# A two-block transformer kernel on one core: who rounds the pooled parts, who copies the queries' columns, where one weights' split stands, and filler products at the beginning

## The chip, the core and the metric

The kernel runs on one core of a Trainium2 chip. The core's engines work from queues of their own: TensorE (PE, with its weight loads shown as PEld), VectorE (DVE), ScalarE (ACT), GpSimd (POOL) and SyncE (SP, which here only issues transfers). They meet at semaphores. The metric is the time of the whole program in microseconds (us), and lower is better.

## What is computed

The program is two blocks, one after the other, on 512 tokens of width 1024. The first block is a gated feed-forward, a mixer and another gated feed-forward. The mixer is what the change touches:

```python
h = rms_norm(x, mix_norm[l])
proj = h @ w_in[l]
q, k, v, qi, ki, wi, u = jnp.split(proj, split_points, axis=-1)
q = rope(rms_norm(q.reshape(B, S, N_HEADS, HEAD_DIM), q_norm[l]), pos, HEAD_DIM)
k = rope(rms_norm(k.reshape(B, S, N_HEADS, HEAD_DIM), k_norm[l]), pos, HEAD_DIM)
attn = dsa_attention(q, k, v, qi, ki, wi, top_k)      # softmax over the 128 best keys by qi, ki, wi
pooled = jnp.einsum('bsgc,gcd->bsgd', multiscale_pool(u), pool_w[l])
pooled = pooled.reshape(B, S, POOL_WIDTH) * pool_scale[l]
x = x + jnp.concatenate([attn, pooled], axis=-1) @ w_out[l]
```

The second block (two attentions with gates, then a convolved feed-forward) is left as it was. All data are 32-bit floats; the large products are made of three products of a high and a low part, which need both operands rounded (the high part) and their remainders (the low part).

## The kernel before

**Weights.** They come through four slots of 1024 columns. SP loads a slab into `raw`, ACT rounds it into `wH` (`split`, L1757 to L1768), POOL makes the remainder `wL` (L806), and PE multiplies. A product of stage and slab needs all three.

**The beginning.** PE waits for the identity matrix and a gain vector, transposes the first half of `x` (L1092, 4 transposes for each of 4 token tiles, each tile when its transfer has landed), then multiplies 4 feature tiles (`first_slabs`). For each feature tile `k` ACT makes the high part (L1804) and DVE the low part (L2310) and a copy of `x` (L2306). PE goes on to the second half of `x` and its four feature tiles. POOL fills constants first, `ones` among them (L794).

**The first attention** has 32 units, `n = 8 * tile + head`. Each engine walks the same units in program order, written by hand (`first_attention` on PE, ACT and DVE):

- PE at an even unit makes the logits of units n+2 and n+3 (`logit_pair`); then it turns the probabilities of unit n (`turn`, L1455), multiplies those of unit n-1 with the values, and runs its `during1(n)`.
- ACT takes the exponential of unit n+1 (L1954), copies the turned probabilities of unit n out of PSUM (L1971), and runs its `during1(n)`.
- DVE masks the logits of unit n+2 (L2613); at units 9, 17 and 25 it normalises the tile before (L2634, L2636); then it runs its `during1(n)`. There it also picks the best keys of the last tile at every even unit from 2 to 20 (`pick`, L2561 and L2562).

In `during1` stand two side jobs. **Pooled parts:** `POOL_AT = {1: 0, 6: 1, 9: 2, 14: 3}` says at which unit PE makes pooled product g into PSUM bank 5 (`pool_product`). ACT rounds it into `hidH` at the same unit (`pool_high`, L1939), and DVE makes the remainder `hidL` two units later (`pool_low`, L2590). All four products use bank 5, and so the next one, and every turn of queries into bank 5, waits for the remainder of the one before (semaphore `hid_ready`). **Tiles of queries and keys:** at units 4, 12 and 20 (`TILE_TURN`) PE turns the next tile's queries and keys (L1405), and ACT copies both out of PSUM, the queries' columns first and the keys' second (`tile_columns`, L1935). The next tile's logits wait for both.

At unit 9 ACT also splits the last slab (slot 3) of the weights that follow the attention (`out1`).

Of the kernel before, what the change touches and what calls it, by code (L numbers as in the profile page):

```python
# [143 lines left out]
def _build(nc, t, stack):  # L144
# [229 lines left out]
    def sem(name):  # L374
        return stack.enter_context(nc.semaphore(name))
# [39 lines left out]
    exp_begun = sem("exp_begun")  # L415
    qk_sq, qk_rot, qk_T, qk_out = sem("qk_sq"), sem("qk_rot"), sem("qk_T"), sem("qk_out")
    att_qk, q2_rot, q2_T, q2_hi, q2_lo, k2_hi = (sem(n) for n in ("att_qk", "q2_rot", "q2_T", "q2_hi", "q2_lo", "k2_hi"))
# [138 lines left out]
    def highs_to(what, n):  # L556
# [40 lines left out]
                   ("conv_w2", t["conv_w_2"][0, 2])]  # L597
    VEC_DMAS = len(vec_sources) - 1

    def prob_of(n):  # L600
# [369 lines left out]
    def _(pe):  # L970
# [120 lines left out]
        def x_block(k, q):  # L1091
            return nc.tensor.transpose(bank(X_BANK[k], P, q * P), xnat[:, q * D + k * P:q * D + (k + 1) * P], ident)  # L1092

        pe.wait_ge(const_in, 16)
        pe.wait_ge(gain_in, 16)
        nc.tensor.transpose(bank(1, KT), vec_rows[0:KT, 0:P], ident[0:KT, 0:KT]).then_inc(gain_T, 1)
        for q in range(ST - 1):
            pe.wait_ge(x_in[q], 16)
            for k in range(4):
                x_block(k, q)  # L1100
        pe.wait_ge(x_in[ST - 1], 16)
        for k in range(4):
# [273 lines left out]
        def before_v():  # L1376
            pe.wait_ge(drained_a, drain_base["k"] + 4)
            pe.wait_ge(k_scaled, 1)

        def pool_product(g):  # L1380
            if g < 2:
                pe.wait_ge(v_late, g + 1)
            if g == 0:
                pe.wait_ge(pooled, 4)
                pe.wait_ge(misc_in, MISC_DMAS * 16 + 16)
            if g >= 1:
                pe.wait_ge(hid_ready, NF + g)
                pe.wait_ge(qk_out, (2, 4, 4, 6)[g])
            product(bank(POOL_BANK[g]), pool_w[:, g * P:(g + 1) * P], u_pool[:, g * S:(g + 1) * S],
                    True, True).then_inc(pool_mm, 1)  # L1390

        def tile_turn(q):
            if q:
                pe.wait_ge(qk_out, 2 * q)
            if q > 1:
# [17 lines left out]
        def during1(n):  # L1413
# [5 lines left out]
            if n in EARLY_TURN:  # L1419
                if EARLY_TURN[n] == 0:  # L1420
                    pe.wait_ge(hid_ready, NF + 4)
                    pe.wait_ge(attn_out, GROUPS1 - 1)
                    pe.wait_ge(qk_out, 2 * ST)
                attn1_turn(EARLY_TURN[n], range(ST - 1))
# [11 lines left out]
        def logit_pair(n):  # L1436
            if n >= 4:
                pe.wait_ge(logit, n - 2)
            if n % NH == 0:
                pe.wait_ge(qk_out, 2 * (n // NH + 1))  # L1440
            for u in group1[n:n + 2]:
# [301 lines left out]
    def _(act):  # L1743
# [185 lines left out]

        def tile_columns(q):  # L1930
            into = (qT1[:, q % 2 * 4 * P:][:, 0:4 * P].rearrange("p (a s) -> p a s", a=4),
                    kT1[:].rearrange("p (a s) -> p a s", a=4)[:, :, q * P:(q + 1) * P])
            for n, b in enumerate(TURN1_BANK[q]):
                act.wait_ge(qk_T, 2 * q + n + 1)
                nc.scalar.activation(into[n], bank(b).rearrange("p (a s) -> p a s", a=4), ACT.Copy).then_inc(qk_out, 1)  # L1935

# [5 lines left out]
        def during1(n):  # L1942
            if n in TILE_TURN:
                tile_columns(TILE_TURN[n])
            if n in POOL_AT:
                pool_high(POOL_AT[n])
            if n == 9:
                split(stage_of["out1"], 0, SLOTS - 1)
# [8 lines left out]
        def first_units():  # L1957
            tile_columns(0)
            exps(0)
            exps(1)  # L1960
# [300 lines left out]
    def _(dve):  # L2261
# [331 lines left out]
        def during1(n):  # L2593
            if n - 2 in POOL_AT:
                pool_low(POOL_AT[n - 2])
            if n in PICK_AT:
                pick(3, 6 + PICK_AT.index(n), 7 + PICK_AT.index(n))
# [566 lines left out]
```

## Time and profile before

| | |
|---|---|
| median of 3 runs | 1738.71 us (1737.01 to 1739.12) |
| the profiled execution's own time | 1738.32 us |
| its span, first to last instruction | 1736.5 us |
| busy: PE / PEld / DVE / ACT / POOL | 98% / 80% / 56% / 38% / 54% |
| share of the last-ended chain on PE | 91% |
| span of the first attention's units | about 507.6 to 562 us |

### The profile page before, as it was taken

The page shows a single profiled execution, that of the slowest core. Times are in us where ns is not written, and L with a number is a line of the kernel's source. Part 1 is how long each engine was busy: PE and PEld are TensorE (multiplying, and loading weights), DVE is VectorE, ACT ScalarE, POOL GpSimd, SP SyncE. Part 2 cuts the span into 40 slices and gives each one's busy share as a digit, 9 for nine tenths or more (in the row PEclk, how much of TensorE's full clock was granted, in tenths as well). Part 3 has the DMA queues.
Part 4 walks back from the last instruction along what each step waited for, and adds up shares of the span by engine and source line. Part 5 has one row for each costly group of instructions (what it writes and reads, how often), then busy time and mean ns, then how long its engine had stood idle before and what let it go on. Part 6 is the DMA issues. An engine that isn't in the chain of part 4 may idle for free.

```text
span 1736.5 us, 24431 instructions
## 1 busy us (share of the span) xinstructions
PE 1705.2 (98%) x8123; PEld 1388.1 (80%) x8123; DVE 977.5 (56%) x1507; ACT 665.8 (38%) x1382; POOL 930.2 (54%) x755
## 2 busy tenths in 40 slices
PE   8999999999999999999999999999999999999997
PEld 7888888888777888888888888864478988888887
DVE  4258645768985467352123529578767673542544
ACT  5322222343466433223223323665632642332333
POOL 4554453567982445544444545467943755544541
PEclk9999999999999999999999999999999999999998
DMA  7354452534211346523423433100122234333321
GB/s 236 109 179 148 146 158 85 176 93 133 73 49 49 122 146 189 150 86 98 126 83 86 122 97 89 33 1 25 49 61 85 71 93 140 97 97 98 97 85 49
DMA packets 279967, 178.39 MB, mean 103 GB/s; under 512 B 6537, under 2 KB 258629, under 8 KB 279749
## 3 DMA queue, kind: packets, MB, share of 16 engines
q1 hardware_dynamic: 265620, 149.36, 29.9%
q10 hardware_dynamic: 14256, 27.87, 4.7%
q8 instruction: 52, 0.85, 0.2%
q14 instruction: 39, 0.31, 0.1%
HBM read 175.11 MB, written 2.10 MB: 102 GB/s over the span
## 4 chain that ended last, share of the span: by engine, by line
PE 91%; DVE 5%; ACT 1%; issue 1%; DMA 1%; POOL 1%; SPq 0%; DVEq 0%; ACTq 0%; POOLq 0%
PE ps L973 89%; DVE mod_acc L2345 2%; PE ps L1455 1%; DVE stat L2662 0%; DVE ps L2688 0%; PE ps L1280 0%; DMA mod_raw<-in_w_mod 0%; DMA xnat<-in_x 0%; POOL wL L806 0%; PE ps L1660 0%; ACT prob2B L2091 0%; POOL actL L860 0%; DVE x L2388 0%; PE ps L1405 0%; PE ps L1154 0%
## 5 line engine op out<-in xcount | busy, mean ns | idle before, releaser
L806 POOL TENSOR_TENSOR wL<-raw,wH 128x512 fp32r<-128x512 f32 (+2 forms) x560 | 747.4, 1358 | 709.1 <-ACT wH L1768 698.1
L973 PE MATMUL ps<-actH,wH 128*128 128x512 f32 (+1 forms) x1312 | 510.6, 389 | 2.6 <-POOL actL L860 1.9
L973 PE MATMUL ps<-actH,wL 128*128 128x512 f32 (+1 forms) x1312 | 503.6, 384 | 0.0
L973 PE MATMUL ps<-actL,wH 128*128 128x512 f32 (+1 forms) x1248 | 480.0, 385 | 0.0
L1768 ACT ACTIVATE wH<-raw 128x512 fp32r<-128x512 f32 (+2 forms) x558 | 311.1, 608 | 295.5 <-PE ps L973 295.4
L973 PEld LDWEIGHTS ps<-actH,wH 128*128 128x128 f32 x1312 | 247.1, 188 | 53.5 <-issue 2.4
L973 PEld LDWEIGHTS ps<-actH,wL 128*128 128x128 f32 x1312 | 246.4, 188 | 49.1
L973 PEld LDWEIGHTS ps<-actL,wH 128*128 128x128 f32 x1248 | 235.1, 188 | 46.7 <-DVE actL L2310 0.8
L973 PE MATMUL ps<-hidH,wH 128*128 128x512 f32 (+1 forms) x720 | 267.6, 372 | 0.0
L973 PE MATMUL ps<-hidH,wL 128*128 128x512 f32 (+1 forms) x720 | 266.6, 370 | 0.0
L973 PE MATMUL ps<-hidL,wH 128*128 128x512 f32 (+1 forms) x720 | 266.5, 370 | 0.0
L973 PEld LDWEIGHTS ps<-hidH,wL 128*128 128x128 f32 x720 | 135.6, 188 | 23.2
L973 PEld LDWEIGHTS ps<-hidH,wH 128*128 128x128 f32 x720 | 135.7, 188 | 23.0
L973 PEld LDWEIGHTS ps<-hidL,wH 128*128 128x128 f32 x720 | 135.7, 188 | 22.8
L2345 DVE SCALAR_TENSOR_TENSOR mod_acc<-mod_raw,silu_c,mod_acc 128x512 f32<-128x512 f32 x112 | 119.5, 1067 | 3.9
L1841 ACT ACTIVATE sg<-g 128x512 f32<-128x512 f32 x44 | 27.8, 632 | 209.7 <-DVE g L2368 209.7
L2370 DVE TENSOR_TENSOR ur<-ps,rB 128x512 f32<-128x512 f32 x44 | 30.3, 690 | 123.4 <-PE ps L973 123.4
L973 PE MATMUL ps<-wH,actH 128*128 128x512 f32 (+1 forms) x224 | 85.2, 381 | 0.0
L973 PE MATMUL ps<-wL,actH 128*128 128x512 f32 (+1 forms) x224 | 84.7, 378 | 0.0
L973 PE MATMUL ps<-wH,actL 128*128 128x512 f32 (+1 forms) x224 | 84.6, 378 | 0.0
L1845 ACT ACTIVATE hidH<-h 128x512 f32 (+1 forms) x44 | 27.7, 630 | 127.2 <-DVE h L2373 127.2
L2388 DVE SCALAR_TENSOR_TENSOR x<-ps,x 128x512 f32 (+1 forms) x32 | 21.6, 690 | 88.0 <-PE ps L973 86.8
(378 smaller groups left out, 2039.8 us busy)
## 6 DMA issues: line engine op xcount, KB each, us to landing
mod_raw<-in_w_mod ACTq DMA_DIRECT2D x24, 1024.0 KB, 6.1
raw<-in_w_in SPq DMA_DIRECT2D x48, 512.0 KB, 3.7
raw<-in_ffn_w_up SPq DMA_DIRECT2D x44, 512.0 KB, 3.8
raw<-in_w_up SPq DMA_DIRECT2D x44, 512.0 KB, 3.9
raw<-in_ffn_w_gate SPq DMA_DIRECT2D x43, 512.0 KB, 3.8
raw<-in_ffn_w_down SPq DMA_DIRECT2D x32, 512.0 KB, 4.0
raw<-in_w_out SPq DMA_DIRECT2D x16, 512.0 KB, 3.8
raw<-in_w_down SPq DMA_DIRECT2D x16, 512.0 KB, 3.8
```

The source lines that it names most:

```text
L806: nc.gpsimd.tensor_tensor(wL[:, b:b + w // 2], raw[:, b:b + w // 2], wH[:, b:b + w // 2].bitcast(F32), ALU.subtract).then_inc(lo_ready, 1)
L973: return nc.tensor.matmul(out, a, b, start=first, stop=last)
L1455: mm = nc.tensor.transpose(into, prob_of(n)[:, b * P:(b + 1) * P], ident)
L1768: nc.scalar.activation(wH[:, b:b + w // 2], raw[:, b:b + w // 2], ACT.Copy).then_inc(hi_ready, 1)
L1841: nc.scalar.activation(sg[:], g1[:], ACT.Silu).then_inc(silu_ready, 1)
L1845: nc.scalar.activation(tile(hidH, f), h[:], ACT.Copy).then_inc(h_high, 1)
L2345: ins = V.scalar_tensor_tensor(o, w, s, o, ALU.mult, ALU.add)
L2370: V.tensor_tensor(ur[:], bank(2 * q + 1), rB[:], ALU.mult).then_inc(drained_v, 1)
L2388: V.scalar_tensor_tensor(tile(x, m), bank(j), 0.5, tile(x, m), ALU.mult, ALU.add).then_inc(drained_v, 1)
```

## The change

1. At the beginning PE makes products of `ones` with `ones` into bank 3, which nobody reads: six before it waits for the identity matrix, and one after each of the first three token tiles' transposes.
2. ACT rounds a pooled part one unit later (`n - 1 in POOL_AT`), and DVE makes its remainder one unit later (`n - 3`). PE makes the products at the same units as before.
3. At units 4, 12 and 20 DVE copies the queries' columns, and ACT the keys' alone. The first tile stays with ACT. The semaphore `qk_out` becomes two, `q_cols` and `k_cols`.
4. The split of slot 3 moves from unit 9 to unit 22.

```diff
+        def awake(n):
+            for _ in range(n):
+                product(bank(3, P), ones[:], ones[:], True, True)
+
+        pe.wait_ge(cleared, 2)
+        awake(6)
         pe.wait_ge(const_in, 16)
...
             for k in range(4):
                 x_block(k, q)
+            awake(1)
         pe.wait_ge(x_in[ST - 1], 16)
...
+        def columns_out(tiles):
+            pe.wait_ge(q_cols, tiles)
+            pe.wait_ge(k_cols, tiles)
...
             if g >= 1:
                 pe.wait_ge(hid_ready, NF + g)
-                pe.wait_ge(qk_out, (2, 4, 4, 6)[g])
+                columns_out((1, 2, 2, 3)[g])
...
-        def tile_columns(q):
-            into = (qT1[:, q % 2 * 4 * P:][:, 0:4 * P].rearrange("p (a s) -> p a s", a=4),
-                    kT1[:].rearrange("p (a s) -> p a s", a=4)[:, :, q * P:(q + 1) * P])
-            for n, b in enumerate(TURN1_BANK[q]):
-                act.wait_ge(qk_T, 2 * q + n + 1)
-                nc.scalar.activation(into[n], bank(b).rearrange("p (a s) -> p a s", a=4), ACT.Copy).then_inc(qk_out, 1)
+        def key_columns(q):
+            act.wait_ge(qk_T, 2 * q + 2)
+            nc.scalar.activation(kT1[:].rearrange("p (a s) -> p a s", a=4)[:, :, q * P:(q + 1) * P],
+                                 bank(TURN1_BANK[q][1]).rearrange("p (a s) -> p a s", a=4), ACT.Copy).then_inc(k_cols, 1)
...
         def during1(n):
             if n in TILE_TURN:
-                tile_columns(TILE_TURN[n])
-            if n in POOL_AT:
-                pool_high(POOL_AT[n])
-            if n == 9:
+                key_columns(TILE_TURN[n])
+            if n - 1 in POOL_AT:
+                pool_high(POOL_AT[n - 1])
+            if n == 22:
                 split(stage_of["out1"], 0, SLOTS - 1)
...
         def during1(n):
-            if n - 2 in POOL_AT:
-                pool_low(POOL_AT[n - 2])
+            if n - 3 in POOL_AT:
+                pool_low(POOL_AT[n - 3])
+            if n in TILE_TURN:
+                q = TILE_TURN[n]
+                dve.wait_ge(qk_T, 2 * q + 1)
+                V.tensor_copy(query_columns(q), bank(TURN1_BANK[q][0])).then_inc(q_cols, 1)
             if n in PICK_AT:
                 pick(3, 6 + PICK_AT.index(n), 7 + PICK_AT.index(n))
```

PE at the beginning, after the change (before it, the rows with `ones` are missing and the 16 transposes stand in one row; `const` is the identity matrix):

```order
L978 MATMUL ps<-ones 128x128 x6
L1107 MATMUL ps<-const,vec_rows 128x8
L1097 MATMUL ps<-const,xnat 128x128 x4
L978 MATMUL ps<-ones 128x128
L1097 MATMUL ps<-const,xnat 128x128 x4
L978 MATMUL ps<-ones 128x128
L1097 MATMUL ps<-const,xnat 128x128 x4
L978 MATMUL ps<-ones 128x128
L1097 MATMUL ps<-const,xnat 128x128 x4
```

Nine products were added, all ahead of the last four transposes.

DVE in the first attention before, from the logits of unit 10 (written to `prob_1`, in the program's unit 8) to the pick of unit 10. `hidL` is the remainder of a pooled part, here of part 1; `small` and `work` belong to the pick; `RECIPROCAL` and `attn` are the normalising of tile 0:

```order
L2613 ISA prob_1_106,stat<-ps,work 128x256
L2613 ISA stat 128x1
L2590 SCALAR_TENSOR_TENSOR hidL<-ps,cols,hidH 128x512
L2561 MAX small<-work 128x8
L2562 MATCH_REPLACE work<-small,work 128x512
L2613 ISA prob_2_107,stat<-ps,work 128x256
L2613 ISA stat 128x1
L2634 RECIPROCAL stat<-stat 128x8
L2636 TENSOR_TENSOR attn_104<-ps,stat 128x512
L2613 ISA prob_0_105,stat<-ps,work 128x256
L2613 ISA stat 128x1
```

The same place after the change:

```order
L2633 ISA prob_1_106,stat<-ps,work 128x256
L2633 ISA stat 128x1
L2577 MAX small<-work 128x8
L2578 MATCH_REPLACE work<-small,work 128x512
L2633 ISA prob_2_107,stat<-ps,work 128x256
L2633 ISA stat 128x1
L2654 RECIPROCAL stat<-stat 128x8
L2656 TENSOR_TENSOR attn_104<-ps,stat 128x512
L2606 SCALAR_TENSOR_TENSOR hidL<-ps,cols,hidH 128x512
L2633 ISA prob_0_105,stat<-ps,work 128x256
L2633 ISA stat 128x1
```

The remainder of part 1 moved behind a pick, the logits of unit 11 and both instructions of the normalising.

ACT before, from the exponential of unit 10 (in the program's unit 9) to that of unit 12. `hidH` is the rounding of part 2, `wH` the split of slot 3:

```order
L1954 ACTIVATE prob_1_106,stat<-prob_1_106,stat 128x256
L1971 ACTIVATE probT_108<-ps 128x256
L1939 ACTIVATE hidH<-ps,cols 128x512
L1768 ACTIVATE wH<-raw 128x512 x2
L1954 ACTIVATE prob_2_107,stat<-prob_2_107,stat 128x256
L1971 ACTIVATE probT_108<-ps 128x256
L1954 ACTIVATE prob_0_105,stat<-prob_0_105,stat 128x256
```

And after the change:

```order
L1968 ACTIVATE prob_1_106,stat<-prob_1_106,stat 128x256
L1987 ACTIVATE probT_108<-ps 128x256
L1968 ACTIVATE prob_2_107,stat<-prob_2_107,stat 128x256
L1987 ACTIVATE probT_108<-ps 128x256
L1953 ACTIVATE hidH<-ps,cols 128x512
L1968 ACTIVATE prob_0_105,stat<-prob_0_105,stat 128x256
```

The rounding moved behind one exponential and one copy, and the two halves of the split are gone from here.

## Rows read from the trace of the kernel before

**Rows 1.** The page: span, and busy time of each engine.

```profile
span 1736.5 us, 24431 instructions
PE 1705.2 (98%) x8123; PEld 1388.1 (80%) x8123; DVE 977.5 (56%) x1507; ACT 665.8 (38%) x1382; POOL 930.2 (54%) x755
```

**Rows 2.** Timeline at the beginning: start us, length us, engine, instruction [idle before].

```profile
1.22 0.20 POOL L794 MEMSET ones<- 128x128 f32 x1
4.05 0.24 PE L1096 MATMUL ps<-const,vec_rows 8*128 8x8 f32 x1 [4.05 <-DMA vec_rows<-in_ffn_norm]
7.18 0.71 PEld L1092 LDWEIGHTS ps<-const,xnat 128*128 128x128 f32 x4 [0.54 <-DMA xnat<-in_x]
7.76 0.69 ACT L1804 ACTIVATE actH<-ps,gain 128x512 fp32r<-128x512 f32 x1 [3.25 <-PE ps L1092]
...
9.74 2.06 DVE L2310 SCALAR_TENSOR_TENSOR actL<-ps,gain,actH 128x512 fp32r<-128x512 f32 x3
...
11.72 1.88 DVE L2306 COPY x<-ps 128x512 f32<-128x512 f32 x3
...
13.90 2.42 ACT L1804 ACTIVATE actH<-ps,gain 128x512 fp32r<-128x512 f32 x4 [1.24 <-PE ps L1092]
```

**Rows 3.** Timeline of PE at the change of its clock.

```profile
12.41 0.63 PE L973 MATMUL ps<-actL,wH 128*128 128x512 f32 x1
12.84 2.33 PE L1092 MATMUL ps<-const,xnat 128*128 128x128 f32 x16
14.93 1.18 PE L973 MATMUL ps<-actH,wL 128*128 128x512 f32 x4
```

**Rows 4.** Stretches: length, busy us of PE PEld DVE ACT POOL, granted clock, DMA.

```profile
525.70:529.11 3.41, 3.41 (x18) 3.32 (x17) 1.89 (x7) 2.02 (x6) 3.41 (x3) 0.50 0.69 207
522.29:525.70 3.41, 2.14 (x17) 1.63 (x17) 2.83 (x9) 2.82 (x10) 3.41 (x4) 1.00 0.00 1
```

**Rows 5.** Timeline of DVE, units 8 and 9 of the first attention.

```profile
518.30 0.75 DVE L2590 SCALAR_TENSOR_TENSOR hidL<-ps,cols,hidH 128x512 fp32r<-128x512 f32 x1
...
521.05 0.69 DVE L2636 TENSOR_TENSOR attn<-ps,stat 128x512 f32<-128x512 f32 x1
```

**Rows 6.** Timeline of PE, units 9 to 14.

```profile
520.15 1.08 PE L973 MATMUL ps<-u_pool,pool_w 128*128 128x512 f32 x2
521.16 0.70 PE L973 MATMUL ps<-kT,qT 64*128 64x256 f32 x4
...
523.89 0.41 PE L1455 MATMUL ps<-const,prob 128*128 128x128 f32 x2 [1.27 <-ACT probT L1971]
...
526.12 1.06 PE L1405 MATMUL ps<-const,q 128*128 128x128 f32 x4
...
529.14 0.92 PE L973 MATMUL ps<-kT,qT 64*128 64x384 f32 x4
```

**Rows 7.** Timeline of ACT, units 9 to 12.

```profile
521.26 0.69 ACT L1939 ACTIVATE hidH<-ps,cols 128x512 fp32r<-128x512 f32 x1 [0.92 <-PE ps L973]
521.85 1.14 ACT L1768 ACTIVATE wH<-raw 128x512 fp32r<-128x512 f32 x2
...
523.38 0.37 ACT L1971 ACTIVATE probT<-ps 128x256 f32<-128x256 f32 x1
...
528.08 0.60 ACT L1935 ACTIVATE kT<-ps 128x512 f32<-128x512 f32 x1 [0.26 <-PE ps L1405]
```

**Rows 8.** Timelines of PE and DVE, units 16 and 20 to 24.

```profile
533.47 0.52 PE L1455 MATMUL ps<-const,prob 128*128 128x128 f32 x3 [0.28 <-ACT probT L1971]
...
540.70 0.61 PE L1405 MATMUL ps<-const,q 128*128 128x128 f32 x4
...
540.29 0.69 DVE L2561 MAX8 small<-work 128x8 f32<-128x512 f32 x1
...
542.26 0.56 DVE L2613 CUSTOM_DVE_ANT_0 prob<-ps,work 128x384 f32<-128x384 f32 x1
...
547.03 0.66 PE L1455 MATMUL ps<-const,prob 128*128 128x128 f32 x4
```

More of the change, by code:

```diff
@@ L415, in _build @@
     exp_begun = sem("exp_begun")
-    qk_sq, qk_rot, qk_T, qk_out = sem("qk_sq"), sem("qk_rot"), sem("qk_T"), sem("qk_out")
+    qk_sq, qk_rot, qk_T = sem("qk_sq"), sem("qk_rot"), sem("qk_T")
+    q_cols, k_cols = sem("q_cols"), sem("k_cols")
     att_qk, q2_rot, q2_T, q2_hi, q2_lo, k2_hi = (sem(n) for n in ("att_qk", "q2_rot", "q2_T", "q2_hi", "q2_lo", "k2_hi"))
@@ L598, in _build, with query_columns @@
     VEC_DMAS = len(vec_sources) - 1
+    def query_columns(q):
+        return qT1[:, q % 2 * 4 * P:][:, 0:4 * P]
     def prob_of(n):
@@ L1393, in tile_turn @@
             if q:
-                pe.wait_ge(qk_out, 2 * q)
+                columns_out(q)
             if q > 1:
@@ L1422, in during1 @@
                     pe.wait_ge(attn_out, GROUPS1 - 1)
-                    pe.wait_ge(qk_out, 2 * ST)
+                    columns_out(ST)
                 attn1_turn(EARLY_TURN[n], range(ST - 1))
@@ L1439, in logit_pair @@
             if n % NH == 0:
-                pe.wait_ge(qk_out, 2 * (n // NH + 1))
+                columns_out(n // NH + 1)
             for u in group1[n:n + 2]:
@@ L1957, in first_units @@
         def first_units():
-            tile_columns(0)
+            act.wait_ge(qk_T, 1)
+            nc.scalar.activation(query_columns(0), bank(TURN1_BANK[0][0]), ACT.Copy).then_inc(q_cols, 1)
+            key_columns(0)
             exps(0)
```

## The prediction, made before the changed kernel had run

> **What bounds the kernel now.** I read the page first: PE is busy for 98% of the span, with some 31 us of idle time in all [rows 1]. So a change in the time is a change in PE's idle time, in PE's work, or in PE's clock. Then I read the timeline in the two places that the change touches.
>
> At the beginning PE first works at 4.05 us, and DVE paces it: the low parts of feature tiles 1 to 3 run without a pause from 9.74 to 11.80, then three copies until 13.60 [rows 2]. PE is on its low level all that time. The product at 12.41 and what follows it at 12.84 lie 0.43 us apart, while four products from 14.93 take 1.18 us, with the tail of the last in it, or 0.25 us each [rows 3]. Half of the clock of 2.4 GHz is 1.2 GHz, so the level rose during the 16 transposes between, after PE had worked without a pause since 9.0 us.
>
> In the first attention PE has many small waits. Two stand out. The turn of unit 11 comes at 523.89 after 1.27 us of idleness [rows 6], because ACT had the rounding of pooled part 2 (itself 0.92 us waiting for PE's product) and then 1.14 us of split ahead of the exponential and the copy that PE needs [rows 7]. And in the stretch from 525.70 to 529.11 the granted clock is 0.50, 1.2 GHz, after a stretch in which PE had been busy for 2.14 of 3.41 us [rows 4].
>
> **Part 1, the filler.** `ones` is there at 1.42 [rows 2]. A plain 32-bit product stands in the trace as two passes (the pooled product is `x2` [rows 6]), and I take a pass of 128 columns to be as long as a transpose of 128 columns. Four transposes take 1.06 us at 1.2 GHz and 0.61 at 2.4, the tail of the last, some 0.2 us, with them [rows 6, 8], so that one is 0.215 or 0.108 us. So six products are 12 passes, 12 x 0.215 = 2.6 us, from 1.5 to 4.1. The first useful transpose comes at 4.05 today [rows 2], so they cost at most 0.1 us, and the wait for the transfers of `x` hides that. The three single ones add 3 x 0.43 = 1.3 us. Today PE waits 0.54 us for the last token tile, until 7.18 [rows 2]. If the clock stays low, the last four transposes begin near 8.1 instead, 0.9 us late. If it rises near 6.9, what is left then runs in half the time, and they begin near 7.5, 0.15 to 0.3 us late. I take that: today the rise came after 4.7 us without a pause (9.0 to 13.7), and with the filler PE has none from 1.5 on.
>
> What that buys: DVE's low parts are no faster, so the eighth product can begin no sooner than 11.80 plus the delay of 0.15, and ends at 12.2 instead of 12.84. The 16 transposes take 16 x 0.108 = 1.7 instead of 2.1 us. The first four of them are done at 12.6, so ACT's high part of feature tile 4 moves from 13.90 [rows 2] to 12.75, and DVE's low part to the end of its copies, 13.75, instead of 14.62. PE then stays just behind DVE and is done with this slab 1.2 us sooner. Behind it PE has no idle time worth naming until the modulation chain at 103 us, whose transfer is issued behind PE's work, so that nothing there holds the gain back. Term: -1.2 us, with ends -1.4 (rise at once) and +0.9 (no rise).
>
> **Parts 2 and 4, the pooled parts and the split, units 5 to 11.** What ACT gives back is plain: no rounding and no split between unit 10's work and unit 11's. But bank 5 is one bank. PE's product of part 2, at unit 9, may not start before DVE has made the remainder of part 1. Today that is done at 519.05 and the product begins at 520.15 [rows 5, 6], 1.1 us later. After the change the remainder stands behind the normalising, whose last instruction ends at 521.74 today [rows 5]. The remainder's 0.7 us leave the time ahead of that. The copy of the queries' columns at unit 4 comes in, at 0.65 us, like the three copies that take 1.88 us together [rows 2]. DVE also waits for it there, so that its later instructions are at best where they are now. So the remainder begins near 521.7 and ends near 522.4: PE waits from 520.3 to 522.45. **This is a new wait of 2.1 us.** Behind it on PE stand the pair of logits (1.01 us after the product's start), the turn of unit 10 (0.63 later, 0.4 long like that of unit 11), ACT's copy of it (0.51 from its start to PE's next turn [rows 6, 7]), and then the turn of unit 11: 522.45 + 1.01 + 0.63 + 0.45 + 0.51 = 525.1, against 523.89 today [rows 6, 7]. So the 1.27 us that the split cost are gained, and 1.2 us more than that are lost: +1.2 us at this point. The bounds: 0 if DVE came out of unit 4 so early that the remainder is done by 521.3, and +2.1 if nothing of the split's time came back.
>
> **Part 3, the columns of tiles 2 and 3.** At tile 2 the turn starts 1.2 us later, at 527.4 instead of 526.12 [rows 6]. At 2.4 GHz its eight transposes take 0.9 us instead of 1.7, and ACT copies only the keys, 0.60 us [rows 7], right behind them: the logits of tile 2 can begin at 527.4 + 0.9 + 0.15 (tail) + 0.60 + 0.15 = 529.2, as today (529.14). The lateness is made good here, as far as the clock is high. At unit 16 PE waits 0.28 us for ACT today, behind the rounding of part 3 [rows 8]; that goes: -0.3. At tile 3 the copy on DVE stands ahead of the last pick and of the logits of unit 23. It can't start before the queries are turned, near 541.0 (540.70 + 0.61 less 0.3 [rows 8]); 0.65 for it, and the 1.97 us that the pick and the closing of the mask take today (540.29 to 542.26 [rows 8]) put those logits at 543.6 instead of 542.26. ACT's exponential of unit 23 can then begin at 544.2. Behind it stand a copy, now the two halves of the split (1.14 us), the exponential of unit 24 and the copy of unit 23, four pieces of 0.4 to 0.8 us besides the split, 3.6 us in all, and PE's turn of unit 24 comes at about 547.8 instead of 547.03 [rows 8]: +0.75 us at the end, and from there to the end of the attention PE and ACT take turns without slack. The other user of the split is POOL, whose 2.5 us for slot 3 then end near 549 to 551; PE needs them past 562, so that is hidden. Term for all of the attention at a high clock: +0.75 us, with ends -0.6 and +2.1.
>
> A rule of the Trainium skill bears on the copy. (VectorE: DVE Perf Modes, Why PSUM operands drop a tier, says that an fp32 operand in PSUM holds VectorE to one element a cycle. 512 columns at that page's 0.96 GHz are 0.53 us by estimate, and the rows of like copies agree roughly at 0.63 to 0.69; by the page's figure the term would be 0.1 us smaller.)
>
> **The clock in the attention.** Before, the fall to 1.2 GHz followed one idle time of 1.27 us with small ones around it. Now one of 2.1 us stands a little ahead of that place. I expect a fall again, within some us behind 520.3, and as long as today's, 3.4 us. It takes up to 1.7 us of work from PE; some 0.5 us of that falls into waits that are left. Today's fall is in today's time and I have taken it out above (the turns at tile 2). Term: +1.2 us, with ends 0 and +1.7.
>
> **Sum.** -1.2 + 0.75 + 1.2 = +0.75. The profiled execution took 1738.32 us (span 1736.5 [rows 1]), 0.4 below the median of 1738.71, so that the changed kernel comes to **1739.1 us**.
>
> **Rivals.** (a) *The clock does not fall behind the new wait:* -1.2 + 0.75 = -0.45, 1737.9 us. For it: other waits of 0.4 to 0.9 us on PE in this stage bring no fall today, and the new one comes in one piece with busy work around it. Against: today one of 1.27 us sufficed [rows 4, 6]. (b) *The filler does not lift the clock in time*, so that part 1 doesn't do what it is there for: +0.6 instead of -1.2 (0.9 us late, 0.3 of it back because the later transposes run high): 1740.9 us. For it: the products use only the same constant, and PE may have pauses where the token tiles land late. (c) *The new wait isn't there*, because DVE is early enough at unit 9: then the split's 1.27 us and the fall of the clock (some 1.1 us) are gained as well: 1738.32 - 1.2 - 2.4 = 1734.7 us. Against it stands the order: one pick, one masking and the normalising lie ahead of the remainder, and the normalising ends at 521.74 today. (d) *Slower:* the clock stays at 1.2 GHz or goes to and fro through units 9 to 20, since PE and ACT wait for each other there. Each us at that level costs 0.5; the bound of a measurable loss (3.5 us) is passed at 8 us of low clock, and at 10 us the time is 1737.9 + 5 = 1742.9 us. Against it: today the level came back within 3.4 us, with PE busy throughout [rows 4]. (The Trainium skill bears on this one: TensorE: Matmul & The Clock Gate, A second HAM failure mode, tells of a kernel whose small idle times between groups of products made the clock go to and fro. The trace agrees in one fall, and shows no second.)
>
> **How the numbers follow.** Chances: forecast 0.50, (a) 0.20, (b) 0.12, (c) 0.06, (d) 0.07, anything else 0.05. A measurement of this kernel can tell some 0.2%, 3.5 us, from no change: below 1735.2 is faster, above 1742.2 slower. The forecast, (a) and (b) lie within it. Faster is (c) with a part of the rest, 0.06; slower is (d) and a part of (b), 0.09; the same 0.85. The range of 8 in 10 runs from (a) with a gain of 1.4 us more (the ends of the attention's term) to (b) with half a microsecond: 1736.5 to 1741.4.
>
> **What would show it.** The filler: rows of `ones` from 1.5 to 4.1, transposes 0.11 us apart before the last token tile, and the second half's transposes near 12.2. The new wait: PE idle for some 2 us ahead of the third pooled product, ended by DVE's `hidL`. No split between unit 9 and 11. The clock: a stretch of 0.50 behind that wait. Logits of unit 23 about 1.3 us later against the turn of tile 3. I am wrong if PE has no wait ahead of the third product, if the first attention as a whole isn't 0 to 3 us longer than before, or if the first 100 us are not about 1 us shorter.

## The result, and the profile after

| | before | after |
|---|---|---|
| median | 1738.64 us (1735.45 to 1743.14, 21 runs) | 1741.86 us (1739.22 to 1745.25, 21 runs) |
| ratio after to before | | 1.0017, 95% interval 1.0011 to 1.0023 |
| the profiled execution's own time | 1738.32 us | 1744.24 us |
| its span | 1736.5 us | 1742.5 us |

The changed kernel is slower by 3.0 us on the mean (1.9 to 4.0 by the interval), and by 3.2 us by the medians. That is 0.17%, so it lies inside what the prediction called the same, but the interval does not reach down to no change. The forecast was 1739.1, and the median is 0.5 us above the range that went with it.

The page after, span and busy time, in the columns of [rows 1]:

```profile
span 1742.5 us, 24471 instructions
PE 1711.2 (98%) x8141; PEld 1391.1 (80%) x8141; DVE 978.2 (56%) x1510; ACT 664.2 (38%) x1379; POOL 929.1 (53%) x755
```

PE's busy time and the span both grew by 6.0 us, so that PE is idle for as long as before, 31.3 us. A part of the added busy time is the filler, which stands where PE used to be idle. The rest is work that took longer, and the stretches below show where the clock was low.

**The beginning, after.** PE's timeline, as in [rows 2, 3]:

```profile
1.48 2.93 PE L978 MATMUL ps<-ones 128*128 128x128 f32 x12 [1.48 <-POOL zero L800]
4.34 0.27 PE L1107 MATMUL ps<-const,vec_rows 8*128 8x8 f32 x1
...
7.42 0.60 PE L1097 MATMUL ps<-const,xnat 128*128 128x128 f32 x4
9.06 0.50 PE L978 MATMUL ps<-actH,wH 128*128 128x512 f32 x1 [1.03 <-ACT wH L1815]
...
12.24 1.91 PE L1097 MATMUL ps<-const,xnat 128*128 128x128 f32 x16
...
20.13 0.39 PE L978 MATMUL ps<-actH,wL 128*128 128x512 f32 x1
21.30 0.66 PE L1092 MATMUL ps<-const,vec_rows 128*128 128x128 f32 x4 [0.78 <-DMA vec_rows<-in_conv_w]
```

`vec_rows` holds the constant vectors, which arrive in 15 small transfers. This went as forecast up to the last row. The twelve passes run from 1.48 to just past 4. The granted clock rises at 6.33 us instead of 13.7, and the last token tile's transposes take 0.60 us without a wait. The second half of `x` is turned at 12.24 (forecast: near 12.2; before: 12.84), and by 20 us PE is 1.0 us ahead. Then it waits 0.78 us. The four transposes at the end are those of `vec_rows`, which `vector_turns` puts behind feature tile `k` = 3 of the second slab (`(j, k) == (1, 3)`). Before, they stood there too, at nearly the same time, and without a wait. Here are the same rows of the kernel before:

```profile
21.20 0.39 PE L973 MATMUL ps<-actH,wL 128*128 128x512 f32 x1
21.43 0.60 PE L1087 MATMUL ps<-const,vec_rows 128*128 128x128 f32 x4
21.78 0.48 PE L973 MATMUL ps<-actH,wH 128*128 128x512 f32 x1
```

So 1.0 us of lead became 0.1. It is not that the constants always land just ahead of 21.3 us. The trace records the semaphore updates by which the 15 transfers report that they have landed. The last one recorded came at 19.53 us before, 1.9 us ahead of PE, and PE 1.2 us sooner would still have come behind it. After the change it came at 21.26, 0.04 us ahead of PE's start, although the last of the transfers was issued at 17.8 us in both. (A trace can miss some of the updates.) One thing that differs around it is a transfer of 16 KB in the queue that the profile calls `instruction`. The first line is from the transfers before, between 23.2 and 25 us, and the second from those after, between 18.9 and 20.4:

```profile
q8 instruction: 1, 0.02, 4.0%
q8 instruction: 1, 0.02, 3.6%
```

It starts at 23.39 us before and at 19.17 after. The experiments below come back to it.

**The first attention, after.** PE's timeline, units 9 to 11, as in [rows 6]:

```profile
519.34 0.41 PE L1471 MATMUL ps<-const,prob 128*128 128x128 f32 x2 [0.77 <-ACT probT L1987]
519.59 0.56 PE L978 MATMUL ps<-v,probT 128*128 128x64 f32 x4
522.05 2.07 PE L978 MATMUL ps<-u_pool,pool_w 128*128 128x512 f32 x2 [1.91 <-DVE hidL L2606]
524.06 1.23 PE L978 MATMUL ps<-kT,qT 64*128 64x256 f32 x4
525.21 0.69 PE L1471 MATMUL ps<-const,prob 128*128 128x128 f32 x2
525.70 0.95 PE L978 MATMUL ps<-v,probT 128*128 128x64 f32 x4
526.47 0.66 PE L1471 MATMUL ps<-const,prob 128*128 128x128 f32 x2
```

The timeline of DVE at the same place, as in [rows 5]:

```profile
520.42 0.20 DVE L2654 RECIPROCAL stat<-stat 128x8 f32<-128x8 f32 x1
520.65 0.69 DVE L2656 TENSOR_TENSOR attn<-ps,stat 128x512 f32<-128x512 f32 x1
521.26 0.74 DVE L2606 SCALAR_TENSOR_TENSOR hidL<-ps,cols,hidH 128x512 fp32r<-128x512 f32 x1
```

The new wait is there, and for the reason given: the remainder `hidL` stands behind the normalising, and the third pooled product needs bank 5 from it. PE idles for 1.91 us. ACT has neither a rounding nor a split between units 10 and 11 any more, and PE's turn of unit 11, at 526.47, is ready without a wait. But its products are long: the pair of the pooled product takes 2.07 us, and 1.08 in [rows 6]. The stretches say why. Columns are length, busy us of PE, PEld, DVE, ACT and POOL, granted clock, DMA share and GB/s, as in [rows 4]:

```profile
518.33:521.74 3.41, 1.04 (x9) 0.80 (x7) 3.31 (x10) 2.34 (x8) 3.25 (x4) 1.00 0.00 0
521.74:525.15 3.41, 3.10 (x6) 1.01 (x6) 0.26 (x1) 0.00 (x0) 3.41 (x3) 0.50 0.00 0
525.15:528.57 3.42, 3.42 (x18) 2.98 (x16) 2.23 (x7) 2.31 (x7) 3.42 (x4) 0.50 0.65 189
528.57:531.98 3.41, 3.41 (x19) 3.02 (x16) 1.71 (x5) 0.39 (x1) 0.44 (x1) 0.50 0.81 240
531.98:535.40 3.42, 3.25 (x20) 2.07 (x20) 3.32 (x11) 2.81 (x9) 0.00 (x0) 1.00 0.10 31
```

The clock is at 1.2 GHz from 521.74 to 531.98, 10.24 us, and not for 3.4 us as in [rows 4]. PE was busy for all but 0.3 us of that. Against the kernel before, the same instructions are 0.03 us early at 500 us, 0.27 us early at 506 us (just ahead of the attention), 4.32 us late at 560 us (behind it), and as late at 900. A second fall, at 1166.86 in the second block's attention, which the change doesn't touch, adds 1.7.

**Unit 23**, as in [rows 8]. The first row is of DVE, the others of ACT and PE:

```profile
544.82 0.69 DVE L2615 COPY qT<-ps 128x512 f32<-128x512 f32 x1 [0.81 <-PE ps L1421]
...
547.39 0.56 DVE L2633 CUSTOM_DVE_ANT_0 prob<-ps,work 128x384 f32<-128x384 f32 x1
...
548.98 1.14 ACT L1784 ACTIVATE wH<-raw 128x512 fp32r<-128x512 f32 x2
...
549.22 0.52 PE L1471 MATMUL ps<-const,prob 128*128 128x128 f32 x3 [0.91 <-ACT probT L1987]
```

The two rows apart are DVE's copy and the logits of unit 23. The copy takes 0.69 us, the masking of unit 23 begins 2.57 us after its start, 3.2 us behind the turn of tile 3 (1.6 before, [rows 8]), and PE idles 0.91 us ahead of its turn of unit 23. The split comes behind that and delays nothing that PE waits for: its next turn follows without a wait ended by ACT.

### The profile page after: what moved, and what is told of

It reads as the page before. It is cut to its first block, busy times and chain, and to the rows that moved or that the text cites. A ratio compares the mean times of both kernels' runs of the same rounds, so it can differ in the third digit from the quotient of the medians.

```text
span 1742.5 us, 24471 instructions
## 1 busy us (share of the span) xinstructions
PE 1711.2 (98%) x8141; PEld 1391.1 (80%) x8141; DVE 978.2 (56%) x1510; ACT 664.2 (38%) x1379; POOL 929.1 (53%) x755
## 4 chain that ended last, share of the span: by engine, by line
PE 90%; DVE 5%; issue 1%; ACT 1%; SPq 1%; DMA 1%; POOL 1%; DVEq 0%; ACTq 0%; POOLq 0%
PE ps L978 88%; DVE mod_acc L2361 2%; PE ps L1471 1%; DVE stat L2682 0%; DVE ps L2708 0%; PE ps L1292 0%; SPq L752 0%; DMA mod_raw<-in_w_mod 0%; SPq L773 0%; POOL wL L811 0%; PE ps L1421 0%; PE ps L1676 0%; ACT prob2B L2107 0%; POOL actL L865 0%; DVE x L2404 0%
## 5 line engine op out<-in xcount | busy, mean ns | idle before, releaser
L978 PEld LDWEIGHTS ps<-hidH,wL 128*128 128x128 f32 x720 | 135.6, 188 | 23.2
L2404 DVE SCALAR_TENSOR_TENSOR x<-ps,x 128x512 f32 (+1 forms) x32 | 21.5, 689 | 88.1 <-PE ps L978 87.3
```

Of the source, the lines that this page charges most:

```text
L978: return nc.tensor.matmul(out, a, b, start=first, stop=last)
L2404: V.scalar_tensor_tensor(tile(x, m), bank(j), 0.5, tile(x, m), ALU.mult, ALU.add).then_inc(drained_v, 1)
```

## The experiments

All numbers of "lead" are differences between the start of the same PE instruction in a kernel's trace and in that of the kernel before; negative is earlier. What the attention costs is read from 506 to 560 us. At 500.07 us PE waits for `q` from DVE, and a kernel that comes there early or late gains or loses up to 0.4 us, which belongs to the stage ahead. Where a kernel has 11 runs, its time stands beside 15 or 33 runs of the kernel before on the same chip.

### The beginning: E1 and E2

E1 is the kernel before with the filler alone. E2 has the filler, and the turns of the constants' rows two feature tiles (six products) later:

```diff
+        pe.wait_ge(cleared, 2)
+        awake(6)
...
-                    if (j, k) == (1, 3):
+                    if (j, k) == (1, 5):
```

> The kernel before with the filler products alone. Theory 1 (the clock rises early and the first half slab is done 1.0 us sooner, but PE then waits for the transfer of the last constant vectors near 21.3 us, ahead of the four transposes of vec_rows, and gives the gain back): transposes of vec_rows at 21.3 to 21.4, time within 0.3 us of before. Rival (the gain of 1.0 us goes through, and what was lost after the change was lost later): 1.0 us less than before.

> The kernel before with the filler, and with the transposes of the constant vectors two feature tiles later on PE. Theory 1: no wait for the constants' transfer, PE is 1.0 us ahead of before at 30 us and still at 95 us, time 1.0 us less than before. Rival (another constraint of the first 100 us holds the beginning, such as the row scale's chain): less than 0.3 us.

Measured: E1 1737.32 us (1736.00 to 1741.13), ratio 0.9996 (0.9987 to 1.0005); E2 1737.21 (1736.43 to 1741.18), 0.9997 (0.9988 to 1.0006). Neither can be told from no change by its time. The traces tell them apart. PE in E1, and then in E2:

```profile
20.14 0.39 PE L973 MATMUL ps<-actH,wL 128*128 128x512 f32 x1
21.38 0.66 PE L1087 MATMUL ps<-const,vec_rows 128*128 128x128 f32 x4 [0.85 <-DMA vec_rows<-in_conv_w]
```

```profile
21.30 0.40 PE L973 MATMUL ps<-actH,wL 128*128 128x512 f32 x1
21.54 0.60 PE L1087 MATMUL ps<-const,vec_rows 128*128 128x128 f32 x4
21.89 0.47 PE L973 MATMUL ps<-actH,wH 128*128 128x512 f32 x1
```

In E1 PE waits 0.85 us at the constants, and its lead at 500 us is -0.03. In E2 it doesn't wait for them, and leads by 1.3 us from 24 us and by 1.5 at 500 us. So in these two the gain is lost at the constants and nowhere else.

The other runs below have the same beginnings, so that all thirteen profiles can be read together. The middle columns are the last recorded landing of the constants and the start of the 16 KB transfer; "lead" is that of PE:

| beginning | profiles | last landing | 16 KB transfer | PE's wait | lead at 20 us | lead at 24 us |
|---|---|---|---|---|---|---|
| no filler | before, E3, E4, E5 | 19.53 to 19.89 | 23.4 to 23.8 | none | -0.46 to +0.33 | -0.48 to +0.33 |
| filler, turns in place | after, E1, E6, E7, E9, E10 | 20.96 to 21.50 | 18.2 to 19.2 | 0.19 to 0.88 | -1.30 to -0.41 | -0.38 to +0.17 |
| filler, turns later | E2, E8, E11 | 19.64 to 19.76 | 19.37 to 19.43 | none | -1.25 to -1.11 | -1.28 to -1.12 |

The filler is worth 0.85 us at 20 us (the mean of nine profiles less the mean of four), a part of it by chance of when the clock rises. With the turns in place nothing of it is left at 24 us, and with the turns later all of it. The constants landed late only where the 16 KB transfer started by 19.2 us, in six profiles of six, and in none of the other seven. That this transfer is PE's code, which the added instructions and the moved turns shift, and that it holds the constants up, fits the rows but is not shown. E2 moved both at once, PE's use of the constants and the 16 KB transfer, and doesn't part them: its constants had landed at 19.64 us, ahead of where PE would have met them without the move.

E2's profile had a fall of the clock in the second attention (at 1159.53), E1's had none. So the profiled executions hide the difference between the two. That the filler makes the kernel faster is not shown by any run's time.

### The parts of the attention, one by one: E3, E4, E5

E3 moves the split alone (`if n == 9` to `if n == 22` in ACT's `during1`). E4 moves the rounding and the remainders of the pooled parts alone (`n - 1 in POOL_AT` on ACT, `n - 3` on DVE). E5 gives the queries' columns to DVE alone:

```diff
+            if n in TILE_TURN:
+                q = TILE_TURN[n]
+                dve.wait_ge(qk_T, 2 * q + 1)
+                V.tensor_copy(query_columns(q), bank(TURN1_BANK[q][0])).then_inc(q_cols, 1)
```

> The kernel before with the split of slot 3 at unit 22 alone. Theory (the split at unit 9 costs 1.27 us of PE's idle time and brings the clock's fall, a further 1 us): 1.0 to 2.5 us less than before, no idle time over 0.9 us ahead of the turn of unit 11, and no stretch at 0.50. Rival (at unit 22 it costs as much as it did at unit 9): within 0.3 us of before.

> The kernel before with the rounding and the remainder of the pooled parts one unit later alone. Theory 2 (the remainder of part 1 behind the normalising makes PE wait 2 us and more for bank 5, and the clock falls after it): a wait of 1.5 to 2.5 us ahead of the third pooled product, ended by DVE's hidL, a longer stretch at 0.50, and 2 to 4 us more than before. Rival (the copies on DVE are what makes it late): a wait below 1 us and within 1 us of before.

> The kernel before with the copies of the queries' columns of tiles 1 to 3 on DVE alone. Theory 2 (the copies push DVE back by 1.2 us behind each turn of a tile, but DVE's remainder of part 1 still stands ahead of the normalising): no wait over 0.5 us ahead of the third pooled product, the logits of unit 23 about 1 us later against the turn of tile 3, PE behind by 0.3 to 0.9 us at the end of the attention against a run of before with the same clock; time 0 to 1 us more than before. Rival (the copies are the main loss): 2 us or more than before.

Measured: E3 1736.74 us (1735.97 to 1739.04), ratio 0.9993 (0.9984 to 1.0002). E4 1740.25 (1739.32 to 1742.41), 1.0013 (1.0004 to 1.0022). E5 1738.10 (1737.01 to 1741.99), 1.0003 (0.9994 to 1.0012). PE's turn of unit 11 in E3, PE's third pooled product in E4, and PE's turn of unit 23 in E5:

```profile
521.72 0.41 PE L1455 MATMUL ps<-const,prob 128*128 128x128 f32 x2 [0.24 <-ACT probT L1971]
```

```profile
524.65 1.12 PE L973 MATMUL ps<-u_pool,pool_w 128*128 128x512 f32 x2 [2.08 <-DVE hidL L2590]
```

```profile
545.29 0.52 PE L1464 MATMUL ps<-const,prob 128*128 128x128 f32 x3 [0.91 <-ACT probT L1980]
```

Each wait of the changed kernel is owned by one part of the change. The late split takes away the 1.27 us that [rows 6] show ahead of unit 11. In the traces it is the one part of the attention's change that gains, though E3's interval still holds no change. The late remainders make the wait of some 2 us, and are the one part that measurably loses. (E4 moves ACT's rounding too; E6 parts the two.) The copy on DVE makes the 0.91 us at unit 23, and costs 0.8 us of lead between 506 and 560 us.

### The changed kernel with one thing put back or covered: E6 and E7

E6 is the changed kernel with the remainders at their old units. E7 keeps them late and gives PE work in the wait: 9 products of `ones` with `ones`, 18 passes, into a part of PSUM that nobody reads:

```diff
-            if n - 3 in POOL_AT:
-                pool_low(POOL_AT[n - 3])
+            if n - 2 in POOL_AT:
+                pool_low(POOL_AT[n - 2])
```

```diff
+            if g == 2:
+                for _ in range(9):
+                    product(bank(7, P, 3 * P), ones[:], ones[:], True, True)
```

> The changed kernel with one edit undone: DVE makes the remainders two units after the product again, ahead of the normalising, while ACT's rounding stays one unit late. Theory 2 (the place of the remainder behind the normalising is the cause): no wait over 0.5 us ahead of the third pooled product, no stretch at 0.50 within 5 us behind it, and 3 us or more less than the changed kernel: 1736.5 to 1738.5. Rival (DVE is late anyway, through the copies): a wait of 1 us or more, and less than 1 us gained on the changed kernel.

> The changed kernel with nine more products of ones (2 us at the high clock) on PE just ahead of its wait for the third pooled product, into a part of a bank that later products overwrite. The wait for DVE is not touched, PE only works through it. Theory 3 (half or more of the loss is the low clock that follows PE's idle time): no or one stretch at 0.50 in the attention instead of three, the third product at the same place within 0.2 us, and 1.5 to 3.5 us less than the changed kernel (1738.5 to 1740). Rival (the low clock is the reason of little, since ACT and DVE pace this part anyway): within 0.7 us of the changed kernel.

Measured: E6 1736.87 us (1735.00 to 1738.96), ratio 0.9991 (0.9982 to 1.0000). E7 1740.16 (1738.85 to 1742.31), 1.0015 (1.0006 to 1.0024). By the medians that is 5.0 us less than the changed kernel for E6 and 1.7 less for E7, by the means 4.7 (3.6 to 5.8) and 1.1 (0.1 to 2.0). E6 is clear. E7 is not: the kernel before was also 0.5 us faster on E7's chip, and its ratio of 1.0015 stands beside 1.0017 with overlapping intervals. What E7 tells, it tells by its trace, and by the mean clock of its runs (below). PE in E6, and PE and two stretches in E7:

```profile
519.06 0.41 PE L1471 MATMUL ps<-const,prob 128*128 128x128 f32 x2 [0.78 <-ACT probT L1987]
519.31 0.56 PE L978 MATMUL ps<-v,probT 128*128 128x64 f32 x4
519.70 1.08 PE L978 MATMUL ps<-u_pool,pool_w 128*128 128x512 f32 x2
...
522.34 0.41 PE L1471 MATMUL ps<-const,prob 128*128 128x128 f32 x2 [0.17 <-ACT probT L1987]
```

```profile
519.48 2.23 PE L978 MATMUL ps<-ones 128*128 128x128 f32 x18
521.55 1.12 PE L978 MATMUL ps<-u_pool,pool_w 128*128 128x512 f32 x2
```

```profile
518.30:521.74 3.44, 2.90 (x25) 2.90 (x26) 3.09 (x8) 1.87 (x8) 3.28 (x4) 1.00 0.00 0
521.74:525.15 3.41, 3.24 (x20) 1.97 (x21) 1.78 (x5) 1.44 (x5) 3.41 (x4) 1.00 0.03 9
```

E7 parts the wait from the fall of the clock. In it the third pooled product is late by as much as in the changed kernel, behind the same remainder, but PE is busy meanwhile and the clock stays at 2.4 GHz. PE then loses 0.91 us between 506 and 560 us (-0.78 to +0.13) against the kernel before, whose own trace has a fall there. The changed kernel lost 4.59 us there (-0.27 to +4.32), so that in its profile 3.7 us were the clock's. E6 has neither the wait nor a fall in the attention, and gains 1.5 us there.

### Does the fall repeat? E9 and E10

The changed kernel as it is, profiled twice more.

> The changed kernel as it is, profiled a second time. Theory (the wait ahead of the third pooled product brings the fall of the clock, every time): a wait of 1.8 to 2.5 us at 522 us, and the granted clock at 0.50 directly behind it, for 3.4 to 10.3 us. Rival (the fall in the attention comes at random and stood there in one execution by chance): the wait is there, and no stretch of 0.50 within 10 us behind it.

> The same a third time. Theory: as in the second. If the fall is there each time but its length differs (one, two or three stretches of 3.41 us), the length is what a prediction can't tell from one trace, and is the reason for a part of the scatter of the times. Rival: no fall behind the wait.

Measured: 1740.69 and 1742.28 us. PE at the third pooled product, of E9 and then of E10:

```profile
522.25 2.07 PE L978 MATMUL ps<-u_pool,pool_w 128*128 128x512 f32 x2 [1.91 <-DVE hidL L2606]
```

```profile
522.51 1.53 PE L978 MATMUL ps<-u_pool,pool_w 128*128 128x512 f32 x2 [1.91 <-DVE hidL L2606]
```

The stretches from the fall on, of E9 and then of E10:

```profile
522.24:525.65 3.41, 3.40 (x7) 1.25 (x8) 0.14 (x1) 0.00 (x0) 3.41 (x4) 0.50 0.01 3
525.65:529.06 3.41, 2.88 (x22) 2.24 (x21) 3.17 (x10) 2.62 (x8) 3.41 (x3) 1.00 0.73 213
```

```profile
523.10:526.51 3.41, 3.41 (x13) 1.90 (x12) 1.25 (x5) 0.66 (x2) 3.41 (x4) 0.50 0.11 31
526.51:529.92 3.41, 2.99 (x25) 2.46 (x25) 2.24 (x7) 2.03 (x7) 2.99 (x3) 1.00 0.82 235
```

The wait is 1.91 us in all three profiles, and the fall stands behind it in all three, but it lasts 10.24 us once and 3.41 us twice. The first profile was the expensive one. With the fall of 3.41 us the attention costs 2.49 us (E9, -0.08 to +2.41) and 2.16 (E10, +0.18 to +2.34), which is E7's 0.91 and 1.6 or 1.3 for the fall. E10 had a second fall in the second attention (1.7 us), E9 none.

Now all profiles can be read together. "Loss" is the change of lead from 506 to 560 us, "fall" what the clock did between 508 and 562 us:

| kernel | longest wait of PE in units 1 to 24 | fall | loss |
|---|---|---|---|
| before | 1.27 (split) | 3.41 us, at 525.70 | 0 |
| E5 | 1.27 (split) | 3.41 us, at 524.91 | +0.82 |
| E1 | 1.27 (split) | none | -1.36 |
| E2 | 1.27 (split) | none | -1.33 |
| E3, E8 | below 0.7 | none | -2.31, -2.33 |
| E6, E11 | 0.91 | none | -1.50, -1.48 |
| E7 | 0.91 (the other is filled) | none | +0.91 |
| E4 | 2.08 (remainder) | 6.83 us, at 512.97, ahead of it | +2.38 |
| after, E9, E10 | 1.91 (remainder) | 10.24, 3.41, 3.41 us, behind it | +4.59, +2.49, +2.16 |

E1 and E2 have the same code in the attention as the kernel before and no fall, and are 1.36 and 1.33 us shorter there: that is what a fall of 3.41 us costs. Two things follow. The kernel before is a reference with a fall in it. Without a fall on either side, the change costs 2.3 us in the attention (E7's +0.91 against -1.36), and the late split by itself gains 1.0 (E3 against E1 and E2).

Behind the wait of 1.27 us a fall came in two of four profiles and behind the wait for the remainder in three of four. In the five kernels without a wait of 1 us none came. But E4's fall, at 512.97, was ahead of its long wait, with no wait over 0.5 us finished in the attention and PE busy for 2.53 of the 3.41 us before. So a long wait is not needed for a fall, and that it makes one likely rests on these few profiles.

The runs that were not profiled say more, by the mean granted clock that each of them has. It is 0.9948 on average over the 21 runs of the changed kernel and 0.9946 over E4's 11. It is 0.9957, 0.9958 and 0.9957 over the 33, 33 and 15 runs of the kernel before on the three chips of the experiments, 0.9960 over E7's 11 and 0.9965 over E6's. A fall of 3.41 us in 1742 us is 0.0010. So the kernels with the late remainder and an empty wait have on average one such fall more in a run than the kernel before, and those in which the wait is filled or gone have not. (The averages are good to some 0.0007 over 11 or 21 runs, and to 0.0003 over 33.)

### Versions of it: E8 and E11

E8 is the kernel before with the filler, the turns of the constants' rows two feature tiles later, and the split at unit 22. E11 is the changed kernel with the two losses taken out, the remainders at their old units and the turns two feature tiles later.

```diff
-                    if (j, k) == (1, 3):
+                    if (j, k) == (1, 5):
...
-            if n == 9:
+            if n == 22:
```

> The kernel before with the filler, the transposes of the constant vectors two feature tiles later, and the split at unit 22; pooled parts and copies as before. All theories: the gains add, 1.2 us at the beginning and 1.3 us in the attention, with a part of the clock's fall: 1735 to 1736.5, that is 2 to 3.4 us less than before.

> The changed kernel with its two losses taken out: the remainders of the pooled parts on DVE a unit earlier (where they were before), and the turns of the constants' rows at the fifth product instead of the third. Theory (additive): 1736.9 of the kernel with the remainders earlier, less the 1.2 us that the constants' transfer gave back at 21 us: 1735.7, a ratio of 0.998 to the kernel before; no wait ahead of the third pooled product, and PE 1.2 us ahead of the kernel before from 24 us on. Rival (the gain at the beginning is lost in waits for DVE and ACT of the attention, or in falls of the clock elsewhere): 1736.5 to 1737.5, the same as the kernels with the one or the other.

Measured: E8 1736.52 us (1734.28 to 1738.69), ratio 0.9990 (0.9981 to 0.9999). E11 1735.47 (1735.28 to 1738.39), 0.9991 (0.9982 to 1.0000). E11's median is 2.9 us below that of the kernel before beside it (1738.35), but it stands at the edge of a group, and the mean is 1.7 us below: six of its eleven runs lie between 1735.28 and 1735.47, five between 1737.37 and 1738.39. PE in E11 at the two places:

```profile
21.57 0.60 PE L1092 MATMUL ps<-const,vec_rows 128*128 128x128 f32 x4
...
518.79 1.08 PE L978 MATMUL ps<-u_pool,pool_w 128*128 128x512 f32 x2
```

Neither wait is left, PE leads by 1.22 us at 500 us and by 2.77 at 900, and the clock never falls before the tail. Both beat the changed kernel by 5 us on the mean. Against the kernel before they gain 1.7 and 1.6 us by the ratios, E8 just clear of no change and E11 not quite. E11 and E8 can't be told apart by their intervals. In the traces E8 is 1.0 us ahead of E11 at 560 us, and the two differ there in the copy of the queries' columns, which E5 priced at 0.8, and in ACT's rounding a unit later.

## Why the prediction came out as it did

| term | forecast | measured |
|---|---|---|
| filler, at 506 us | -1.2 | -0.3, -0.1, +0.2 (after, E9, E10); -0.4 (E1); -1.5, -1.4, -1.3 (E2, E8, E11, turns later); no filler: 0, -1.2, 0.0, -0.4 (before, E3, E4, E5) |
| attention at a high clock, against before with its fall | +0.75 | +0.9 (E7) |
| fall of the clock | +1.2 | +3.7, +1.6, +1.3 (after, E9, E10, less E7) |
| sum | +0.75 | +4.3, +2.4, +2.3, and 1.7 for a fall in the second attention in after and E10 |

- **What bounds it: right.** The time is PE's idle time and PE's clock, and every term was found there.
- **The filler up to 20 us: right, the size in the first profile only.** Rows of `ones` to 4, the rise at 6.33, the second half's transposes at 12.24, 1.06 us of lead. In E9 and E10 the rise came at 6.8 and 7.7, and the lead was 0.76 and 0.41.
- **The step that failed:** "Behind it PE has no idle time worth naming until the modulation chain at 103 us", so "nothing there holds the gain back". PE waited 0.78 us for the constants ahead of 21.30 (0.45 and 0.37 in E9 and E10, 0.85 in E1), and of the 1.2 us at most 0.3 is left at 506 us. This is the missing 1.2 us of the sum: with 0 in place of -1.2 it gives 1740.3, and E2 keeps its lead past this place. What was wrong is not only that a semaphore was overlooked. In the trace of before the constants' last recorded landing is at 19.53, so that a look at it would still have given the gain free passage. The step took it that transfers land in the changed kernel as they did in the kernel before, and these landed 1.4 to 2.0 us later wherever the filler stood and the turns hadn't moved. Why they did stays open; the 16 KB transfer is the one suspect that the traces show.
- **The new wait: right**, in its place, its reason and its size (forecast PE idle from 520.3 to 522.45, measured 1.91 us of idleness up to 522.05). DVE's remainder ran from 521.26, 0.4 us sooner than I took it. What the attention costs at a high clock comes out by E7, +0.9 for +0.75. That this is so little is because the fall of before is in the reference, as the prediction said; without it the cost is 2.3 us.
- **Unit 23: the place right.** The copy on DVE costs 0.8 us (E5), as forecast for the end of the attention. The logits of unit 23 came 1.6 us later against the turn of tile 3 (forecast 1.3). The split, which the prediction added in there, delays no turn.
- **The fall of the clock: the place right, the amount too small.** It came in all three profiles behind the new wait. Two of them lost 1.6 and 1.3 for a fall of 3.41 us, near the term. The third fell for 10.24 us and lost 3.7. Rival (d) had 8 to 10 us of low clock: that is what the first profile shows, from the fall's length and not from going to and fro, and at less than its half a microsecond for each. What the term left out is that the low clock of one run is not that of the next: the changed kernel's runs have on average one fall more than those of the kernel before, where the prediction had one in place of one. (The Trainium skill, TensorE: Matmul & The Clock Gate, A second HAM failure mode, which the prediction weighed for that rival, describes an oscillation through small idle times. No profile of the changed kernel shows one: each has one fall behind the wait, and then 2.4 GHz until the next block, though waits of 0.4 to 0.9 us go on.)
- **The reference point.** The profile of before had a fall of its own in the attention, and E1 and E2 show that this is not in every execution. As a number the reference was sound: the profiled execution lies 0.3 us below the median of 21 runs.
- **The rivals.** (a), no fall, is E7 or E6 and not the changed kernel. (b), no lift of the clock, didn't happen. (c), no new wait, is what E6 makes of it: 1736.87, not 1734.7, since the filler's gain is lost there too. E11, which keeps it, has 1735.47.

With 0 for the filler and the measured 0.9 and 1.3 to 1.6 for the attention and its fall the sum gives 1740.5 to 1740.8. E9, the profile with just one fall, has 1740.69. The median is 1741.86. The runs of the changed kernel lie in two groups, ten from 1739.22 to 1740.63 at a mean clock of 0.995 to 0.997, eleven from 1741.86 to 1745.25 at 0.991 to 0.995. So the rest is more time at a low clock, in falls like those at 1165 and 1167 us or in long ones. What stays open is why the fall behind the wait lasts 3.4 us once and 10.2 another time, where the additional falls of the runs without a profile stand, and what moved the constants' landing.

## What to carry to other kernels

Added instructions can move more than the engine on which they stand. Here nine products on TensorE went with a 16 KB instruction transfer 4 to 5 us sooner and constants that landed 1.4 to 2.0 us later, and a gain of 1 us was gone 8 us after it was made. The trace of the kernel before showed neither. So after an engine is made earlier, follow its lead against the kernel before through the new trace, find where it is lost, and compare the landings of the transfers there in both. An instruction is not moved a step later on an engine without asking which other engine waits for the buffer that it frees; here one unit later on DVE, behind a normalising, held back PE by 2 us and cost more than all the rest gained. And where TensorE waits for 1 to 2 us in the middle of a busy stage, count on a second price in the clock. It is paid in some executions and not in others, so that one profile doesn't give its size, and the profile of the kernel before may have such a fall in it that flatters the change. The mean granted clock of many runs shows it.

## What the runs showed of the hardware

- The granted clock falls behind waits much shorter than the fall: 1.27 us of idleness (before) and 1.91 us (after, E9, E10), with PE busy for 2.14, 1.04, 0.80 and 1.40 of the 3.4 us ahead of the fall, were followed by 3.41, 10.24, 3.41 and 3.41 us at 1.2 GHz. I hadn't expected that the same wait of 1.91 us could bring 3.41 us in one execution and 10.24 in another, in which PE was busy for 9.93 of the 10.24 us. E4's fall of 6.83 us came with PE busy for 2.53 of the 3.41 us ahead of it.
- The same code shows a fall in one execution and none in another (before and E1, units 9 to 13). E1 had 2.13 us of PE busy in the stretch from 521.70, the kernel before 2.14 in its own [rows 4], and only one of them fell.
- A fall of 3.41 us costs 1.3 to 1.7 us on a path that is nearly all PE (E1 and E2 against before 1.36 and 1.33, E9 and E10 less E7 1.6 and 1.3, the second attention 1.7). In the one profile with products of a constant in the wait (E7) it is not there, and the mean granted clock of E7's 11 runs, 0.9960 against 0.9948, agrees.
- The rise at the beginning moved from 13.7 us to between 4.7 and 7.7 us in the nine profiles with the filler, and not to the same moment in any two of the changed kernel's three (6.33, 6.83, 7.69). Without the filler it came at 12.9 twice, at 13.7, and once, in E4, at 7.8 with a fall again at 11.21.
- The same 15 transfers of constants, the last issued at 17.8 to 18.2 us, had their last recorded landing at 19.5 to 19.9 us in seven profiles and at 21.0 to 21.5 in six. The six are those in which a 16 KB transfer of the `instruction` queue started between 18.2 and 19.2 us.
